# Expert stage: routing cut into pieces between dot products, query matmuls spread over the V rows, V gathers issued 24 rows behind the U gathers

## What is computed

```
q = (xi @ wq).reshape(128, 8 heads, 2, 128)
s = einsum('nhcd,hckd->nhck', q, keys)          # 128 keys per half
sv, si = top_k(s, 16)                            # 16 best of each half
cand = sv[:, :, 0, :, None] + sv[:, :, 1, None, :]   # 256 pairs
fv, fi = top_k(cand, 16)                         # 16 experts
eidx = take_along_axis(si0 * 128 + si1, fi)
gw = softmax(fv)
ue = u[eidx];  ve = v[eidx]                      # rows of 1024 floats
act = gelu(einsum('nd,nhkd->nhk', xi, ue))
out = einsum('nhk,nhkd->nd', gw * act, ve)
x = x + gt2 * out
```

## Time and profile before

| | us |
|---|---|
| median of 3 executions | 6892.31 (6862.84 to 6897.56) |
| the profiled execution, its span | 7306.2 |
| busy in it: PE, DVE, ACT, POOL | 5383.4, 3494.9, 1537.5, 3402.7 |
| gathers, U and V | 1280 and 1280, 2560 issues of POOL |

### The profile page before, as it was taken

How to read it: one execution, slowest core, us unless ns; L and a number is a source line. 1 busy time by engine, 2 the same in 40 slices (tenths; PEclk the granted TensorE clock), 3 DMA queues, 4 the chain that set the end, 5 groups by cost and what they waited for, 6 DMA issues and landing times. The chain is left out here.

```text
span 7306.2 us, 69061 instructions
## 1 busy us (share of the span) xinstructions
PE 5383.4 (74%) x25140; PEld 3590.8 (49%) x25140; DVE 3494.9 (48%) x7471; ACT 1537.5 (21%) x3146; POOL 3402.7 (47%) x3088
## 2 busy tenths in 40 slices
PE   5978869957676767677669788699566667676766
PEld 3867768943333333333248677689333333333332
DVE  5154432255555555555452544412555555555553
ACT  4231122111111212121142212321111111111111
POOL 1223321246666666666612233112466666666665
PEclk8988979978888888888979888899788889888888
DMA  5110002168888888888851100021788888888888
GB/s 183 48 37 7 9 28 73 61 242 318 323 313 326 319 326 307 324 321 324 306 188 28 37 7 12 24 76 58 266 331 300 322 317 328 311 318 321 321 324 302
DMA packets 521157, 1531.84 MB, mean 210 GB/s; under 512 B 56478, under 2 KB 154718, under 8 KB 520552
## 3 DMA queue, kind: packets, MB, share of 16 engines
q0 software_dynamic: 369024, 1342.47, 49.2%
q1 hardware_dynamic: 149708, 184.85, 7.7%
q10 hardware_dynamic: 2080, 0.01, 0.0%
HBM read 1522.06 MB, written 5.09 MB: 209 GB/s over the span
## 5 line engine op out<-in xcount | busy, mean ns | idle before, releaser
L1876 PE MATMUL pb<-vb,x_diags 128*128 128x512 f32 x5120 | 2539.1, 641 | 659.8 <-DMA vb<-in_p_v,x_idx 390.9
L1749 DVE CUSTOM_DVE_ANT_0 ub<-ub,h 128x1024 f32<-128x1024 f32 x1280 | 1534.7, 1223 | 1576.2 <-DMA ub<-in_p_u,x_idx 1532.0
L1876 PEld LDWEIGHTS pb<-vb,x_diags 128*128 128x128 f32 x5120 | 985.1, 203 | 2174.3 <-issue 1862.0
L1693 POOL DMA_INDIRECT vb<-in_p_v,x_idx x1280 | 1387.6, 1084 | 793.7 <-PE pb L1876 454.1
L1693 POOL DMA_INDIRECT ub<-in_p_u,x_idx x1280 | 1349.1, 1054 | 756.3 <-issue 374.4
L1827 ACT ACTIVATE x_diags<-identity,x_coefs 128x128 f32<-128x128 f32 x1280 | 469.1, 396 | 1295.0 <-PE pb L1876 1050.3
L1858 PE MATMUL pb<-kT,x_qT 128*128 128x128 f32 x320 | 94.7, 449 | 592.2 <-ACT x_qT L1802 558.1
L250 PE MATMUL pb<-e_Whi,hS_hi 128*128 128x256 f32 x1280 | 382.0, 298 | 27.6 <-DVE e_Wlo L1595 27.4
L1858 PEld LDWEIGHTS pb<-kT,x_qT 128*128 128x128 f32 x320 | 71.8, 312 | 610.3 <-ACT x_qT L1802 575.0
L251 PE MATMUL pb<-e_Wlo,hS_hi 128*128 128x256 f32 x1280 | 360.3, 281 | 0.0
L252 PE MATMUL pb<-e_Whi,hS_lo 128*128 128x256 f32 x1280 | 359.5, 281 | 0.0
(11 more groups left out here) (383 smaller groups left out, 8679.6 us busy)
## 6 DMA issues: line engine op xcount, KB each, us to landing
adaW<-in_ada_w SPq DMA_DIRECT2D x24, 2048.0 KB, 9.3
e_Wg<-in_w_in SPq DMA_DIRECT2D x24, 1024.0 KB, 5.9
ub<-in_p_u,x_idx POOLq DMA_INDIRECT x1280
vb<-in_p_v,x_idx POOLq DMA_INDIRECT x1280
m_W<-in_w_in SPq DMA_DIRECT2D x16, 1024.0 KB, 5.5
Wq<-in_p_wq SPq DMA_DIRECT2D x8, 2048.0 KB, 16.4
g_W<-in_w_in SPq DMA_DIRECT2D x12, 1024.0 KB, 5.1
modAB<-mod_rows SPq DMA_DIRECT2D x16, 512.0 KB, 6.2
```

Source lines behind the costliest of these rows:

```text
L1693: G.indirect_dma_start(ring[:, n % RING, :], None, table, bass.IndirectOffsetOnAxis(ap=idx[:, i % 4, s:s + 1], axis=0)).then_inc(in_[n % R ...
L1749: V.tensor_tensor_reduce(out=ub[:, n % RING, :], in0=ub[:, n % RING, :], in1=h2[:, t, :], scale=1.0, scalar=0.0, op0=ALU.mult, op1=ALU.add ...
L1876: last = mm(pb[2 * (t % 2) + j][:, :], diag[:, n % RING, :], vb[:, n % RING, 512 * j:512 * j + 512], start=(h == 0 and s == 0), stop=(h == ...
```

## The change

The arithmetic and the number of instructions on each engine's data path stay the same. What moves:

- POOL: one loop over rows. Each step issues the U gather of row n and then the V gather of row n - 24 (LAG). Rings of ub and vb stay at 6.
- DVE: `route` becomes a generator with ten `yield`s, so it has eleven pieces. After each dot product of group i from s = 2 on, one piece of route(i+2) runs. coefs(i-1) stands after dot product s = 2 of group i, and `close` after s = 8 of the third group of the next tile.
- PE: the q product of group i+5 (QAHEAD) is split into 16 parts of one matmul, one ahead of each V row of group i. The scores of group i+4 stand ahead of row s = 3.
- ACT: the copy of scores of group i+4 stands after diagonal s = 5; GELU of i+1, weights of i+2 and the copy of q of i+5 stand after diagonal 15.
- The small tiles of a group (indices, weights, dots, coefficients) get 6 slots in place of 4 (LIVE), the diagonals 10 in place of 6 (DRING).

```diff
+        DRING = 10
+        LIVE = 6
+        AHEAD, QAHEAD = 2, 5
+        LAG = 24
...
-                        for s in range(PTOP):
-                            gather(0, s, table_u, ub, u_in, x_dot)
-                        for i in range(NG):
-                            for s in range(PTOP):
-                                if i + 1 < NG:
-                                    gather(i + 1, s, table_u, ub, u_in, x_dot)
-                                gather(i, s, table_v, vb, v_in, x_vmm)
+                        for n in range(PTOP * NG + LAG):
+                            if n < PTOP * NG:
+                                gather(n, table_u, ub, u_in, x_dot)
+                            if n >= LAG:
+                                gather(n - LAG, table_v, vb, v_in, x_vmm)
...
-                        for i in range(NG):
-                            if i + 2 < NG:
-                                route(i + 2)
-                            if i + 1 < NG:
-                                dots(i + 1)
-                                coefs(i + 1)
-                            if i % PH == 1 and i > PH:
-                                close(i // PH - 1)
+                        for i in range(NG):
+                            pieces = route(i + AHEAD) if i + AHEAD < NG else iter(())
+                            for s in range(PTOP):
+                                dot_row(i, s)
+                                if s >= 2:
+                                    next(pieces, None)
+                                if s == 2 and i >= 1:
+                                    coefs(i - 1)
+                                if s == 8 and i >= PH + 2 and i % PH == 2:
+                                    close(i // PH - 1)
+                            whole(pieces)
+                        coefs(NG - 1)
...
-                                if n >= RING:
-                                    act.wait_ge(x_vmm, n - RING + 1)
-                                S.activation(diag[:, n % RING, :], ident[:, :], ACT.Copy, scale=coef[:, i % 4, s:s + 1]).then_inc(x_diag, 1)
+                                if n >= DRING:
+                                    act.wait_ge(x_vmm, n - DRING + 1)
+                                S.activation(diag[:, n % DRING, :], ident[:, :], ACT.Copy, scale=coef[:, i % LIVE, s:s + 1]).then_inc(x_diag, 1)
+                                if s == 5 and i >= 1 and i - 1 + QAHEAD < NG:
+                                    sc_evac(i - 1 + QAHEAD)
                             if i + 1 < NG:
                                 gelu(i + 1)
+                            if i + AHEAD < NG:
+                                weights(i + AHEAD)
+                            if i + QAHEAD < NG:
+                                q_evac(i + QAHEAD)
...
-                            if i + 3 < NG:
-                                q_product(i + 3)
-                                scores(i + 3)
                             for s in range(PTOP):
                                 n = PTOP * i + s
+                                if s == 3 and i >= 1 and i - 1 + QAHEAD < NG:
+                                    scores(i - 1 + QAHEAD)
+                                if i + QAHEAD < NG:
+                                    q_product(i + QAHEAD, s, PTOP)
                                 pe.wait_ge(x_diag, n + 1)
```

More of the change, by code:

```diff
@@ L1667, in stage_experts @@
                 ef = sb(st, "x_ef", [P, PTOP])
[L1668 to L1673, removed]
+                fv = sb(st, "x_fv", [P, LIVE, PTOP])
+                nm = sb(st, "x_nm", [P, LIVE, 3])
+                idx = sb(st, "x_idx", [P, LIVE, PTOP], i32)
+                dot = sb(st, "x_dots", [P, LIVE, PTOP])
+                coef = sb(st, "x_coefs", [P, LIVE, PTOP])
+                diag = sb(st, "x_diags", [P, DRING, P])
                 ybuf = sb(st, "x_y", [P, 512])
@@ L1684, in _, with gather @@
                     def _(pool):
-                        def gather(i, s, table, ring, in_, used):
-                            n = PTOP * i + s
+                        def gather(n, table, ring, in_, used):
+                            i, s = n // PTOP, n % PTOP
                             if s == 0:
@@ L1719, in route @@
                                 link(V.max_index(si[:, 1, o], sv[:, 1, o], rows[1]))
+                                yield
                                 if r == 0:
@@ L1767, in close, with whole @@
                                 dve.wait_ge(x_add, 2 * t + j + 1)
+                        def whole(pieces):
+                            for _ in pieces:
+                                pass
                         for b in range(4):
@@ L1772, in _ @@
                         dve.wait_ge(x_iota, 16)
[L1773 to L1776, removed]
+                        for i in range(AHEAD):
+                            whole(route(i))
                         for i in range(NG):
-                            if i + 2 < NG:
-                                route(i + 2)
-                            if i + 1 < NG:
-                                dots(i + 1)
-                                coefs(i + 1)
-                            if i % PH == 1 and i > PH:
-                                close(i // PH - 1)
+                            pieces = route(i + AHEAD) if i + AHEAD < NG else iter(())
[9 more added lines that the diff above has]
+                        coefs(NG - 1)
                         close(NT - 1)
@@ L1838, in _, with q_product @@
                         pe.wait_ge(x_ke, 4)
-                        def q_product(i):
+                        def q_product(i, part, n_parts):
                             t, h = i // PH, i % PH
[L1842 to L1848, removed]
-                                              start=(k == 0), stop=(k == KD - 1))
-                            last.then_inc(x_q, 1)
+                            if part == 0:
+                                if i < PH and h % 2 == 0:
+                                    pe.wait_ge(wq_in[h // 2], 16)
+                                if i >= 2:
+                                    pe.wait_ge(x_qe, i - 1)
+                            share = 2 * KD // n_parts
+                            for m in range(share * part, share * part + share):
+                                c, k = m // KD, m % KD
+                                last = mm(pb[4 + i % 2][:, c * P:(c + 1) * P], Wq[:, k, (2 * h + c) * P:(2 * h + c + 1) * P], hT[:, k, t * P:(t + 1) * P],
+                                          start=(k == 0), stop=(k == KD - 1))
+                            if part == n_parts - 1:
+                                last.then_inc(x_q, 1)
                         def scores(i):
@@ L1859, in scores @@
                             last.then_inc(x_s, 1)
-                        for i in range(3):
-                            q_product(i)
+                        for i in range(QAHEAD):
+                            q_product(i, 0, 1)
                             scores(i)
```

46 lines of the change are left out of this document (23 added, 23 removed).

## The result

| | before | after |
|---|---|---|
| median, us | 6894.94 (6862.84 to 6907.05, 4 runs) | 6516.31 (6498.56 to 6558.35, 4 runs) |
| span of the profiled execution | 7306.2, recorded again 6871.0 | 6502.2 |

The ratio is 0.947, 95% interval 0.943 to 0.951 (the two medians alone give 0.945): 5.3% less, where the prediction had 3.8% less and a range of 6330 to 6790 us. The profiled execution that the prediction was read from was itself no ordinary one: 7306 us of span is 6% above every timed run of the kernel before.

What follows compares the result with a forecast made beforehand. POOL's gather line, held by waits from routing and the q burst, was taken as the bound; 290 us less a layer, 580 in two, gave span 6726, less (414 - 316) a median of 6630 us, 3.8% less; range 6330 to 6790.

Steps and rivals of the forecast that it cites:

- What bounds before: Expert stages: POOL takes 52.8 us a group, 43.7 us of issues and 9 us of waits for DVE and PE.
- (c): Rival: on POOL and DVE, dots and issues collide fully, at most 1.04 us a dot, 7210 us; chance 0.05.
- Routing in pieces: DVE: routing spread over slots 2 to 12 has cover; POOL's dot wait of 3.65 us a group goes.
- Query matmuls spread: PE: one q matmul of 0.23 us ahead of each V row; no gain or cost taken.
- V gathers at 24: Chain from dot 15 to V row 0 has 5 to 6 slots, 14 us; no wait replaces PE's 4.1 us.
- (b): Rival: a new wait in the diagonal chain on ACT and PE, 2 us a group, 6784 us; chance 0.10.
- The pace: Expert stages after: POOL 44.0 us plus 0.5 for PE's slow clock, 44.5 us a group; ends 42.0 and 46.3.
- DMA floor of 42.0 us: Expert-stage gathers: 16.8 MB a group at 399 GB/s, the lower end for a group's time.
- Span and median: Span 7306 - 580 = 6726 us; recording's late q completion, 316 of the 414 us excess, puts the median at 6630.
- (a): Rival: PE's late q completion is there without the profiler too, 6310 us with a group of 44.5; chance 0.28.
- (d): Rival: PE falls to 1.2 GHz and stays, 62 us a group, 7630 us; chance 0.03.
- The signs: Expert stage: dot and L1876 waits nearly gone, 44 to 45 us per 32 issues, DMA share 0.95 or more.

Runs made afterwards that it cites:

- dots_apart: After with the whole routing behind dot 2 and a filler of 0.42 us behind each dot from the third on: 6866.58 us, 0.9982.
- before_pieces: Before with the routing in pieces and nothing else, route(i+3) behind the dots of group i+1: 6687.11 us, 0.9737.
- q_burst: After with the q product of a group in one piece ahead of V row 0: 6526.71 us, 0.9486.
- before_again: The kernel before, recorded again with no edit: 6873.25 us, ratio 0.9992, span 6871.0.
- half_bytes: After with gathers of 2 KB rows in place of 4 KB and dots of the full 1024 columns: 6995.01 us, 1.0169.
- half_dots: After with dot products over 512 of the 1024 columns, gathers whole: 6477.28 us, 0.9435.

## Why the prediction was right, and where it was not

The time fell inside the range, but not by the mechanism that the prediction priced, and in part by luck.

**What bounds before.** The place was right, GpSimd's issue line with DMA engines that could do more (359 against 399 GB/s), and so was the culprit, the whole routing: without it in pieces there is no gain (0.9984). The mechanism was wrong. I priced 9 us a group of waits; in the record that agrees with the timed runs they are 1.2 us, and the loss is 32 x (1.130 - 0.945) = 5.9 us of lengthened issues. I had the row of 1.99 us in hand and used it for the rival (c) alone.

**Routing in pieces.** Its cover on VectorE was right, and `dots_apart` shows that there is more. It isn't the 3.65 us of dot waits that went, but the gathers' length. Alone it brings 2.6%.

**Query matmuls spread.** I took nothing, and it is nothing both ways: 0.9999 in before, 0.9486 against 0.947 when taken out of after.

**V gathers at 24.** No new wait came, so (b) fell. The chain that I timed at 14 us of slack holds at 20 and breaks at 16. I gave the lag no gain of its own. `before_pieces` (0.9737) and `q_burst` (0.9486) both have the pieces and the burst, and between them lies the other half of the gain; they differ by the lag of 24 and by what comes with it (coefs behind dot 2, ten diagonals, six slots, q five groups ahead), which these runs don't part. With the routing whole, all of it and the spread bring nothing, so it works only on top of the pieces. The lag was not tried alone, and why `before_pieces` stays at 377 GB/s rather than 403 is open; its mean issue of 1.058 us says that the even phase isn't held there.

**The pace.** 44.5 us a group was the term that was mis-sized: 41.6 came. The 0.28 us a dot from the stretches without routing was too much for after, whose whole lengthening is 149 / 1280 = 0.12 us a dot. The first record was not at fault in this: the ordinary record of before has 0.33 and 0.21 us a dot in the U rows of the last two groups of each layer, and after has 0.05 and 0.07 there. I took the price of a dot as fixed, and it moves with the phase. The DMA floor of 42.0 us, my lower end, is where it landed: 403 GB/s for 399. With it, per layer: first V issue 14 us later, measured 1588.76 against 1572.29, 16.5; 616 pairs 1713 us, measured 3191.7 - 1588.8 = 1603; 24 V gathers alone 41 us, measured 3231.5 - 3191.7 = 40.

**Span and median.** The span was to be 6726 us and is 6502, 224 less, of which 2 x (1713 - 1603) = 220 are the pace. The median was to lie 98 us below the span and lies 14 above. The two errors have opposite signs, and 114 us are left of them: that the median came out this near is luck, not a sign that either step held. The better argument was at hand: a record 6% above every timed run can't carry prices for single waits.

**The rivals.** (a), a late completion of q that is there without the profiler too: its premise is false, since the copy follows in 0.04 us in 78 of 80 groups both in `before_again` and in `before_pieces`; its number, 6310, is 206 us too low. Whether recording brought it about in the first record, or something else did, isn't known. (c) is false as a full collision but right in kind: half of after's issues start inside a dot and cost little, and as many in `half_bytes` make that kernel slower than before, at 0.50 us a dot and not at 0.8, a bound that I had from the 52.8 us of the first record. It takes a bad phase, not more dots. (d) is false: the clock rose from 0.94 to 1.00 (windows from 2000 to 3000 us).

**The signs.** Waits for dots gone: yes. 32 issues in 44 to 45 us: 41.6. Share over 0.95 at over 375 GB/s: 1.02 at 403. Copy of q within a microsecond: yes. Span and median nearer: 804 us less against 379, but only because the first record was out of line; against 6871.0 the span fell by 369.

## What to carry to other kernels

Compare the profiled execution's time with the timed runs before taking prices from it; when it stands several per cent above all of them, ask for another. Where GpSimd issues gathers while VectorE works on large operands, add up the issues' own lengths, not only the waits: an issue that starts inside such a dot product ends 0.82 us behind the dot's end, one that is under way when the dot starts is not lengthened, and 1280 dots cost 0.12 us each in after and 0.50 us (646 / 1280) in `half_bytes`, by their phase. Fewer bytes can then make a kernel slower, so test a change in the pace of one engine with the phase of the others in view.

## What the runs showed of the hardware

- One core's gathers of 4 KB rows ran at 402 to 409 GB/s in the slices inside a stage of after, with a DMA share of 1.02 in the windows.
- An issue of an indirect gather (0.945 us) that started inside an operation of VectorE with two inputs in SBUF, a dot product or a compare, ended 0.82 us behind that operation's end. One that started inside a sum with one input was not lengthened. The other way round, a dot that started inside an issue was not delayed (1.224 us).
- Half the bytes for each gather (2 KB rows) at the same number of gathers gave 175 to 193 GB/s at a share of 0.62 to 0.68, so a gather of half the bytes kept the DMA engines busy for more than half the time: 0.62 / 665 against 1.02 / 769, 70%.
- A gather's issue on GpSimd took 0.95 us and 0.30 us to the next, for 2 KB rows as for 4 KB: 32 in 40 us, where the DMA engines, when they set the pace (406 GB/s in `half_dots`), needed 41.5 us for the 4 KB rows. The two limits lie 4% apart, which is why small lengthenings decide.
